# A decoder layer step on one core: where the first slabs land, who loads the small inputs, and the order of the opening

## What is computed

```python
shift, scale, gate = split(silu(c) @ w_ada + b_ada, 3)        # c: 1 prompt row, 8 sample rows
h = rmsnorm(x, g_pre) * (1 + scale) + shift                   # 1024 + 8 rows of 1024 columns
hc, bc, cc, gc, q, k, v, ga = split(h @ w_in, 8)              # eight parts of 512 columns
ya = rmsnorm(bc * conv3(cc * hc), g_conv) * silu(gc)
o  = stick_breaking_attention(q, k, v, b_sb)                  # 8 heads of 64; samples read cache_k, cache_v
yb = rmsnorm(o, g_attn) * silu(ga)
y  = x + gate * rmsnorm(concat(ya, yb) @ w_out, g_post)
```

## Time and profile before

| | us |
|---|---|
| median of 3 runs | 855.66 (855.65 to 857.3) |
| the profiled execution | 854.16 |
| its span, first to last instruction | 852.4 |
| TensorE busy | 793.9 (93%) |
| VectorE busy | 542.4 (64%) |
| GpSimd busy | 429.3 (50%) |
| ScalarE busy | 355.2 (42%) |
| mean granted clock of TensorE | 0.985 |

### The profile page before, as it was taken

One profiled execution on the slowest core, in us unless ns is written; L12 is line 12 of the kernel. 1 busy time (PEld: TensorE's weight loads), 2 busy tenths in 40 slices (PEclk: granted clock), 3 DMA queues, 4 the chain that ended last, 5 costly groups with the idle time before them and its releaser, 6 DMA issues. The chain is left out here.

```text
span 852.4 us, 14509 instructions
## 1 busy us (share of the span) xinstructions
PE 793.9 (93%) x4445; PEld 522.7 (61%) x4445; DVE 542.4 (64%) x739; ACT 355.2 (42%) x726; POOL 429.3 (50%) x230
## 2 busy tenths in 40 slices
PE   0799979999999899999989999999899999899995
PEld 0455756766787576668856766778576665343442
DVE  2567669876586688847759776586687854223334
ACT  6311046685222558722146675222467731111122
POOL 0105896374688556566985474688655530100000
PEclk9989999999999999999999999999999999899998
DMA  8999866477779977776898776879977678553101
GB/s 326 335 287 303 261 224 198 142 231 219 247 234 316 290 248 247 221 239 212 291 317 263 230 232 199 259 234 301 326 213 225 197 273 343 159 188 125 50 25 52
DMA packets 131071, 197.85 MB, mean 232 GB/s; under 512 B 10025, under 2 KB 51030, under 8 KB 130994
## 3 DMA queue, kind: packets, MB, share of 16 engines
q1 hardware_dynamic: 99794, 181.20, 64.9%
q10 hardware_dynamic: 31200, 15.73, 6.6%
HBM read 185.25 MB, written 11.66 MB: 231 GB/s over the span
## 5 line engine op out<-in xcount | busy, mean ns | idle before, releaser
L620 POOL TENSOR_TENSOR prod<-ring,qb 128x1024 f32<-128x1024 f32 x128 | 311.4, 2453 | 193.6 <-DMA ring<-in_cache_k_dram 79.8
L1202 DVE TENSOR_REDUCE zd<-prod 128x16 f32<-128x1024 f32 x128 | 154.1, 1213 | 43.8 <-POOL prod L620 43.4
L1348 PE MATMUL ps<-hT,wsl 128*128 128x258 f32 (+1 forms) x640 | 175.3, 420 | 0.0
L1348 PEld LDWEIGHTS ps<-hT,wsl 128*128 128x128 f32 x640 | 119.6, 191 | 54.3 <-issue 19.1
L1348 PE MATMUL ps<-xT,wS 128*128 128x258 f32 x352 | 93.0, 388 | 0.0
L1348 PE MATMUL ps<-ring,apad 128*8 128x512 f32 (+1 forms) x608 | 82.9, 626 | 8.2 <-DMA ring<-in_cache_v_dram 6.4
L1348 PE MATMUL ps<-xT,wsl 128*128 128x258 f32 x352 | 89.5, 386 | 0.6 <-DVE gab L1083 0.6
L662 ACT ACTIVATE av<-ps 128x512 f32<-128x512 f32 (+3 forms) x96 | 46.7, 486 | 87.4 <-PE ps L1591 86.2
L1212 DVE TENSOR_SCALAR zc<-ps,bsb 128x512 f32<-128x512 f32 (+3 forms) x96 | 54.7, 611 | 40.6 <-PE ps L1348 40.4
L1348 PEld LDWEIGHTS ps<-xT,wsl 128*128 128x128 f32 x352 | 62.9, 190 | 20.3 <-issue 11.9
L1348 PEld LDWEIGHTS ps<-xT,wS 128*128 128x128 f32 x352 | 62.7, 192 | 16.3 <-issue 9.5
(11 more groups left out here) (240 smaller groups left out, 1007.5 us busy)
## 6 DMA issues: line engine op xcount, KB each, us to landing
ring<-in_cache_k_dram SPq DMA_DIRECT2D x256, 256.0 KB, 3.7
ring<-in_cache_v_dram SPq DMA_DIRECT2D x256, 256.0 KB, 3.1
wsl<-in_w_in_dram ACTq DMA_DIRECT2D x30, 512.0 KB, 6.8
ring<-in_w_ada_dram SPq DMA_DIRECT2D x6, 2048.0 KB, 11.6
xT<-in_x_prompt_dram SPq DMA_DIRECT2D x2, 2048.0 KB, 10.1
out_dram<-oT SPq DMA_DIRECT2D x8, 512.0 KB, 4.8
ring<-in_x_prompt_dram SPq DMA_DIRECT2D x8, 512.0 KB, 8.0
xT<-y_parts SPq DMA_DIRECT2D x6, 512.0 KB, 9.9
```

The source lines that it names most:

```text
L620: pool.tensor_tensor(prod[:, p % 2].rearrange("p (j c) -> p j c", j=2), kring[:, p % 4], qb[:, p // 16].unsqueeze(1).to_broadcast([P, 2, H ...
L1202: v.tensor_reduce(zd[:, t // 16, :, r:r + 2], prod[:, t % 2].rearrange("p (j h d) -> p h j d", j=2, h=NH), AX_X, ALU.add)\
L1348: return nc.tensor.matmul(out, l, r, start=start, stop=stop, skip_group_check=True)
```

## The change

It touches the opening and the first seven steps of the first group.

- Slab 2 goes to a third home, the four slots of `wsl`, so slabs 0, 1 and 2 are issued without a wait. Slab 3 waits for product 1, the q and k weights for product 2, and slab 4 follows them.
- The nine small inputs are issued by ScalarE, between its instructions for c.
- `ada(2)` stands ahead of group 8, `ada(3)` behind all transposes. The columns of slabs 0 to 2 are made (`modulation(0..2)`) before `ada(3)`, those of slab 3 behind it.
- The columns of `hT` are scaled by VectorE for channel tiles 0 to 3 and by ScalarE for 4 to 7, chunk by chunk. The sample columns come behind VectorE's first chunk.
- TensorE's first projection stands ahead of the query strips, which move into t = 0; `query_rows` moves to t = 1, `gate_strips` to 2 and 6, `gate_sums` to 3 and 7; VectorE's `gates` move to 1 and 6; ScalarE's copies move with them.
- ScalarE's table load at the head of each group is left out.

```diff
-ADA_AT = (6, 14)
+ADA_AT = (8,)
+HK = KT // 2
...
+        ada_slot.append(wsl[:, :, :, :].rearrange("p s k c -> p (s k c)").rearrange("p (k c) -> p k c", k=KT))
+        def ada_at(n):
+            return {0: (0, 1), 1: (1, 1), 2: (2, 1), 3: (1, 2), 4: (0, 2), 5: (1, 3), 7: (1, 4)}[n]
...
-            ADA_FREE = {2: 1, 3: 2, 4: 3, 5: 4, 7: 5}
+            ADA_FREE = {3: 2, 4: 1, 5: 4, 7: 5}
...
             load_ada(0, ada_v[0])
-            sp_e.dma_start(xs, ...).then_inc(small_in, 16)
...
             load_ada(1, ada_v[1])
             load_ada(2, ada_v[2])
             load_ada(3, ada_v[3])
-
-            load_ada(4, w_in[0, :, 2048:2560].rearrange("(k p) c -> p k c", p=P))
+            sp_e.wait_ge(ada_ps, 3)
             for s in range(2):
                 sp_e.dma_start(wsl[:, s, :, :], w_v[PART[s]][0]).then_inc(w_full[s], 16)
+            load_ada(4, w_in[0, :, 2048:2560].rearrange("(k p) c -> p k c", p=P))
...
 ScalarE:
+            act.dma_start(xs, x_sample.rearrange("b l d -> (b l) d")).then_inc(small_in, 16)
...
+            ada_copy(3)
+            act.wait_ge(mods_ready, 1)
+            act.wait_ge(xT_dve, KT)
+            for c in range(3):
+                cols = slice(CH * c, min(CH * (c + 1), SEQ))
+                for k in range(HK, KT):
+                    run(hT[:, k, cols], hT[:, k, cols], ACT.Identity, h_act, scale=mods[:, KT + k, 0:1],
+                        bias=mods[:, k, 0:1])
...
-                act.preload_act_table_set(ACT_SET)
...
+                    if first and t == 0:
+                        query_strips()
+                    if first and t == 1:
+                        query_rows()
...
-                    if first and t in (1, 5):
+                    if first and t in (2, 6):
                         gate_strips(t // 5)
...
 VectorE:
             for c in range(3):
                 cols = slice(CH * c, min(CH * (c + 1), SEQ))
-                for k in range(KT):
+                for k in range(HK):
...
-                    if first and t in (0, 5):
+                    if first and t in (1, 6):
                         gates(t // 5)
...
 TensorE:
+            pe.wait_ge(ada_copied, 3)
+            for n in range(3):
+                modulation(n)
+            ada(3)
+            pe.wait_ge(ada_copied, 4)
+            modulation(3).then_inc(mod_ps, 1)
...
-                    if first and t in (1, 5):
+                    if first and t in (2, 6):
                         gate_strips(t // 5)
-                    if first and t in (2, 6):
+                    if first and t in (3, 7):
                         gate_sums(t // 6)
```

More of the change, by code:

```diff
@@ L222, in stick_breaking_mixer @@
         x_in = [sem(f"x_in{i}") for i in range(2)]
-        ada_full = [sem(f"ada_full{i}") for i in range(2)]
+        ada_full = [sem(f"ada_full{i}") for i in range(3)]
         w_full = [sem(f"w_full{i}") for i in range(4)]
@@ L698, in _, with query_strips, query_rows @@
                 run(hT[:, n // 2, 0:HALF], ps[:, n % 4, :], ACT.Copy, xT_act)
-            act.wait_ge(qs_ps, 1)
-            run(qsP, ps[:, DB, :], ACT.Copy, qs_copied, scale=HD ** -0.5)
-            act.wait_ge(qs_ps, 2)
-            run(qsP[0:NB, :], ps[0:NB, DB, :], ACT.Copy, qs_copied)
+            ada_copy(3)
[6 more added lines that the diff above has]
+                        bias=mods[:, k, 0:1])
+            def query_strips():
+                act.wait_ge(qs_ps, 1)
+                run(qsP, ps[:, DB, :], ACT.Copy, qs_copied, scale=HD ** -0.5)
+            def query_rows():
+                act.wait_ge(qs_ps, 2)
+                run(qsP[0:NB, :], ps[0:NB, DB, :], ACT.Copy, qs_copied)
             def gate_strips(n):
@@ L1366, in strips @@
             def strips(bank, lhs, n):
-                pe.wait_ge(ada_full[n % 2], 16 * (n // 2 + 1))
+                slot, fill = ada_at(n)
+                pe.wait_ge(ada_full[slot], 16 * fill)
                 for k in range(KT):
                     j = k % 4
-                    last = mm(ps[32 * j:32 * j + 32, bank, :], lhs(k), ada_slot[n % 2][:, k, :], k < 4, k >= 4)
+                    last = mm(ps[32 * j:32 * j + 32, bank, :], lhs(k), ada_slot[slot][:, k, :], k < 4, k >= 4)
                 return last
@@ L1395, in _, with modulation, query_strips @@
             last.then_inc(xT_full, 1)
-            pe.wait_ge(ada_copied, 4)
-            pe.wait_ge(xT_sdve, 1)
-            for k in range(2 * KT):
-                last = mm(ps[:, MB, 256 + 9 * k:265 + 9 * k], ada_cols(P * k, P), e32[:, 0:9], True, True)
-            last.then_inc(mod_ps, 1)
-            pe.wait_ge(h_ready, 1)
-            pe.wait_ge(par_copied, 2)
-            strips(DB, lambda k: hT[:, k, SEQ:NTP], 4).then_inc(qs_ps, 1)
-            pe.wait_ge(ada_copied, 4)
+            def modulation(n):
+                for k in range(4 * n, 4 * n + 4):
+                    last = mm(ps[:, MB, 256 + 9 * k:265 + 9 * k], ada_cols(P * k, P), e32[:, 0:9], True, True)
+                return last
+            pe.wait_ge(xT_sdve, 1)
+            pe.wait_ge(ada_copied, 3)
+            for n in range(3):
+                modulation(n)
+            ada(3)
+            pe.wait_ge(ada_copied, 4)
+            modulation(3).then_inc(mod_ps, 1)
+            def query_strips():
+                pe.wait_ge(h_ready, HK + 1)
+                pe.wait_ge(par_copied, 2)
+                strips(DB, lambda k: hT[:, k, SEQ:NTP], 4).then_inc(qs_ps, 1)
             def gate_strips(n):
@@ L1428, in project_qk @@
                     if part == Q_:
-                        pe.wait_ge(h_ready, 1 + KT * (chunk + 1))
+                        pe.wait_ge(h_ready, HK * (chunk + 1) + (1 if chunk else 0))
+                        pe.wait_ge(h_act, HK * (chunk + 1))
                     if chunk == 0:
```

49 lines of the change are left out of this document (26 added, 23 removed).

## The result

| | before | after |
|---|---|---|
| median, runs side by side | 856.08 us | 864.09 us (863.67 to 865.22) |
| ratio, with its 95% interval | | 1.0093 (1.0076 to 1.0111) |
| profiled execution, and its span | 854.16, 852.4 | 863.67, 862.0 |
| first turn of the attention (E) | 119.61 | 133.13 |
| last turn | 690.43 | 703.60 |

The change made the kernel slower by 8.0 us: the direction of the forecast (+4.7), but at 864.09 just beyond its range, which ended at 864.0. A second series of the changed kernel, on another chip, gave 865.57 against 854.10, a ratio of 1.0137 (1.0110 to 1.0164). So the loss is known only roughly: taken together, the two intervals reach from 6.5 to 14 us.

What follows compares the result with a forecast made beforehand. The main part was taken as bound by TensorE, so a shift carries to the end: S 4.7 us earlier, but a later gate chain moves E from 119.6 to 124.3. 855.66 + 4.7 = 860.4 us, range 854.3 to 864.

Steps and rivals of the forecast that it cites:

- S: Opening: moment the dense work begins, 51.96 before; forecast 47.3, 4.7 us earlier, bounds 46.5 and 49.0.
- the price of the low clock behind the stop: After TensorE's 5.6 us stop at the first gate sum: lower clock, 1.6 us lost.
- Rival C: Opening: ScalarE held by its own DMA issues, S = 54.5, about 867 us; chance 0.09 with other slips in S.
- Their order swaps who pays the 1.4 us; the sum stays.: First projection ahead of query strips: whichever comes first pays the lower clock's 1.4 us, their total unchanged.
- Transposes at 28.6: Opening: transposes start at 31.75 - 3.2 = 28.6, as ScalarE's sample square starts at 18.8 instead of 22.01.
- Modulation at 39.1: Opening: modulation starts at 39.1, after transposes of 7.4, product 2 of 1.92 and sample transposes with copy of about 1.1.
- 2.1 for 24 passes: Opening, modulation of slabs 0 to 2: 24 passes cost 2.1 (full clock) to 3.7 us; 2.1 taken.
- Slab 3's product, 1.92, and all columns by 44.5: Opening: slab 3's product 1.92, its copy 0.65, the last 8 passes 0.7 us, ending at 44.5.
- Scaling: Last columns to first projection: 0.8 us to the first scaling, then 1.9 with VectorE and ScalarE sharing a chunk.
- rival D: Later groups: key loads rather than TensorE set the pace, difference shrinks to 0 to 2 us; chance 0.14 with A.
- A: First gate sum: TensorE's stop partly hidden, time between 855 and 857.4 us; chance 0.14 with rival D.
- B: First gate sum: no stop if GpSimd starts 5.6 us earlier; E = 117.2, 853.2 us; chance 0.09.

Runs made afterwards that it cites:

- a2_after: The changed kernel unaltered, timed again on another chip against the kernel before: 865.57 against 854.10 us, ratio 1.0137.
- e1: Changed kernel with only VectorE's first gate put back to step 0, ahead of the reductions of the first two key products: ratio 1.0071 to the kernel before.
- e10: e9 with the nine small inputs issued by SP again, between slab 0 and slab 1: ratio 0.9988 to the kernel before.
- e3: Changed kernel with slab 3's product ahead of the columns of slabs 0 to 2: ratio 1.0114 to the kernel before.
- e5: Changed kernel with sample columns, query strips and query rows put back ahead of the first projection, gates left late: ratio 1.0013 to the kernel before.
- e6: Changed opening with slab 3's product ahead of all columns, body in old order, all scaling on VectorE: ratio 0.9943 to the kernel before.
- e7: Changed opening with slab 3's product ahead of all columns, old body order, slab 4 issued before q and k weights: ratio 0.9920 to the kernel before.
- e9: Both edits of e6 and e7 together, all scaling on VectorE and slab 4 ahead of the q and k weights: ratio 0.9949 to the kernel before.
- e11: e9 with slab 2 back in the first half of ring, behind product 0 (third home undone): ratio 0.9939 to the kernel before.

## Why the prediction was right and wrong

**Right: the mechanism and the stretch from S to E.** The sum had E - S = 77.0; it is 79.6 and 79.3. In order, each for the traced execution of the result and for a2_after:

| from, to | forecast | after | a2_after |
|---|---|---|---|
| S to GpSimd's first product | 25.5 | 27.2 | 27.4 |
| to the first gate operation ready, TensorE free | 7.1 | 6.5 | 6.5 |
| (TensorE's stop in it) | 5.6 | 6.04 | 6.71 |
| to the second gate sum, K | 31.1 | 32.4 | 31.9 |
| to the first turn, E | 13.3 | 13.5 | 13.5 |

VectorE's gate and memset at K took 4.5 us (120.66 to 125.12) with GpSimd idle, and no operation took 2.5 as one did before. Over the fourteen traces VectorE's second gate operation took 0.68 us with GpSimd idle and 0.68 to 2.81 beside it. That agrees with the rule on the interface shared with VectorE (the Trainium skill, GPSIMD Engine Reference, Specifications) by which the sum had left 1.4 us out. That the shift goes through is right too: +13.5 at the first turn, +13.2 at the last. Rival C is out: ScalarE's DMA issues took 0.25 to 0.61 us each. It was SP that waited, 8.08 us at the issue of a slab behind x and another slab. Too small was the price of the low clock behind the stop: the sum had 1.6 us, e1 shows 2.2 to 2.9, and that is the 0.8 to 1.3 in the row of K.

The largest miss in that table is GpSimd's start, and about half of it or more is one sentence: *"Their order swaps who pays the 1.4 us; the sum stays."* It did not. The strips went from 3.29 to 1.92, but the first projection from 4.89 to 7.1 and 7.6 (6.4 to 7.7 in the five traces in which it stands first; 4.9 to 5.7 in the nine with the strips first). With the projection first TensorE has 3.35 us of idling ahead of it instead of 1.42, and the low stretch is longer. From S to the strips' end it is 9.4 and 9.0 us where the sum had 8.2. The loads, the store and the reload behind it add the other 0.5 and 1.1.

**Wrong: S.** It was to be 47.3, within 46.5 and 49.0; it is 53.50 and 50.23. This is the step that failed, worth 6.2 and 2.9 us: rows that came later than the sample square alone would have them, and TensorE's passes from 39.1 to 44.5 priced at the full clock and too short even for that. Piece by piece:

- *Transposes at 28.6*: they start at 30.07 and 29.73. The sample square was put right behind the last prompt square of before, but that square itself moved by 1.5 us, since the second half of x came at 16.0 instead of 14.48. e10 shows what goes with it: with the small inputs on SP, x is back at 14.38. There SP issues slab 1 at 13.55, behind the long issue; in the change its issue begins at 3.10 and is over by 11.2, beside x. Of the 3.2 us 1.7 to 2.1 came.
- *Modulation at 39.1*: at 40.2 and 40.4, the same lateness and no more. Then *2.1 for 24 passes*: 2.85 at the full clock (a2_after) and 3.79; if half of the 4.89 us for 32 is at the lower clock, 32 take 3.67 at the full one (e3: 3.74) and 24 take 2.75, so that the 2.1 does not follow even from its own premise.
- *Slab 3's product, 1.92, and all columns by 44.5*: they end at 46.9 and 50.1. The bound of 49.0 for S had the low clock over the columns alone. The low clock took in slab 3's product and the last columns too, and that is the 3.3 us between the two traces. The bound of S should have been laid over all work of TensorE up to the next long dense stretch.
- *Scaling*: from the last columns to the projection it is 3.35, where the sum had 2.8. ScalarE's piece took 0.57 and not the 0.46 of the earlier trace rows, a copy out of `ps`: the nearest row was not near.

**In sum.** E was to be 124.3. In a2_after S adds 2.9 and the stretch behind it 2.3, to 129.5; in the traced execution of the result 6.2 and 2.6, to 133.1. Of its +13.5 some +9.5 reached the end, since before's one trace had a tail of 162.0, at the top of the 158.3 to 162.0 of fourteen traces, and after's one of 158.4 (from E to the end 732.8 and 728.9 us, where the forecast had them equal). That is not rival D, whose shift would have shrunk on the way: it was still 13.2 at the last turn. A difference of two single traces is uncertain by that much, and the range had nothing for it.

Rivals A and B are out: the stop was longer, not shorter, and GpSimd came later than in the sum. B had its point, though: e5, where GpSimd starts at 69.97, has no stop and is even with before.

**What stays open.** Why the clock falls during the early columns in one execution and holds in the next, with the same program. One trace of before carries all the differences of E; its own spread in the opening isn't known. ScalarE's table loads are left out in every run but before, so their part is not shown. Between e6, e7, e9 and e11 the runs can't choose: 0.992 to 0.995. All four beat before; e7_slab4_first had the lowest median, 847.75 against 854.10.

## What to carry to other kernels

Moving an operation later in a queue costs what stands behind it on other engines: here eight small matmuls, put behind one projection, delayed a chain of key loads, a store and reload, and GpSimd by some 8 us, and a gate that had been free then stopped TensorE. Ask of each move which chain it starts, and when that chain is wanted. Undo parts one at a time *and* in pairs: the two costs here were not a sum. And take a mark where the two programs have become equal again, and one where the changed stretch begins, behind the same event in both: their distance held to 0.6 us over three traces with the same order, while the times of single runs scattered by 3 us and more.

## What the runs showed of the hardware

- The granted clock isn't settled by the program: slab 3's product, the same instruction behind the same work, took 1.92 us in one trace of the changed kernel and 3.64 in another. Strips or projection, whichever came first behind the last columns and 1.42 to 3.35 us of idling, ran wholly or in part at the lower clock in all fourteen traces (strips 2.75 to 3.64 us against 1.92 in full, projection 6.42 to 7.66 against 4.89). And the fall needs no idling in the record: in before and after it came amid the column matmuls of 9 columns each, with TensorE busy throughout (before 0.97 in 47 to 48 us, 0.50 from 48 on; after 0.50 from 42 on).
- A queue of DMAs that is held up can be a help: SyncE's issue of the sample rows took 7.26 to 7.52 us with x and a slab ahead of it, and with it slab 1 was issued later and the second half of x came 1.2 to 1.9 us sooner. That the one is the cause of the other is argued from e9 and e10, not tried by itself. ScalarE issued the small inputs in 0.25 to 0.61 us each. The Trainium skill, DMA: Bandwidth & Descriptors (Issuing engines are not separate DMA queues), has it that several issuers save issue time only. Here SyncE was through with the small inputs at 13.5 us (e10), ScalarE at 9.1 (after), and the transposes came 0.93 us sooner with it; that the data share the way would fit the later x, but is not shown.
- Slab 2 issued at 11.19 instead of behind the product of slab 0 bought nothing that shows (e9 against e11, S 47.43 and 47.02, E 115.05 and 115.56): slabs 2 and 3 were both there when the transposes were done, but for 0.28 us.
